# Two-block transformer kernel: GpSimd residual held behind a weight remainder, first loads in two pieces, convolution taps redistributed

## The reference, cut to what matters

```python
# layer 0: RWKV-7 time mix, layer 1: causal attention with rotary embedding ("MoBA")
x = layer_norm(ALPHA * x + mixer(x), ln_mix_g, ln_mix_b)
x = layer_norm(ALPHA * x + (silu(x @ w_gate) * (x @ w_up)) @ w_down, ln_ffn_g, ln_ffn_b)
# time mix, its head: six mixes of x with its predecessor
xx = time_shift(x) - x
xr, xw, xk, xv, xa, xg = [x + xx * mu[n] for n in range(6)]
# second block
n = rmsnorm(h);  c_a, c_g, q, k, v, qi, ki, wi, gc, ga = split(n @ w_in)
u = conv31(c_a * sigmoid(c_g))                # 31 taps per channel, causal, depthwise
score = sum_h wi_h * relu(qi_h . ki)          # 8 index heads
keep  = top 64 keys of each query by score    # mask for the attention over q, k, v
h = h + (sig(gc) * conv_out(u) + sig(ga) * attn_out(attention)) @ w_mix
```

## Time and profile before

| | us |
|---|---|
| median of 3 runs | 1421.13 (1420.81 to 1423.71) |
| profiled execution: its own time | 1424.44 |
| profiled execution: span of its instructions | 1422.2 |
| PE busy in the span | 1337.4 |
| DVE busy | 886.6 |
| ACT busy | 604.2 |
| POOL busy | 66.3 |

### The profile page before, as it was taken

The page is one execution under the profiler, slowest core; times in us unless marked ns, Lnnn a source line. Parts: engine busy times, 40 slices in busy tenths (PEclk is TensorE's granted clock), DMA queues, the critical chain, the costliest instruction groups (busy, mean ns, idle before and its releaser), DMA issues.

```text
span 1422.2 us, 20846 instructions
## 1 busy us (share of the span) xinstructions
PE 1337.4 (94%) x8852; PEld 1192.5 (84%) x8852; DVE 886.6 (62%) x1353; ACT 604.2 (42%) x866; POOL 66.3 (5%) x44
## 2 busy tenths in 40 slices
PE   7999999999999999998999998999988987799998
PEld 3687889879999977767999998989887976699997
DVE  5267776585444475556554447989988655555555
ACT  1432233454344444445433445434345535544443
POOL 0021000030000031002000001000000000000000
PEclk9999999999999999999999999989999999899999
DMA  9333000248555554221755655544533452265650
GB/s 291 128 108 134 14 1 1 102 136 266 180 195 188 178 167 159 97 81 60 264 181 179 189 193 163 151 149 148 160 126 105 143 182 85 86 203 190 200 166 30
DMA packets 154525, 205.59 MB, mean 145 GB/s; under 512 B 7456, under 2 KB 128416, under 8 KB 154304
## 3 DMA queue, kind: packets, MB, share of 16 engines
q1 hardware_dynamic: 154432, 204.25, 44.0%
HBM read 203.19 MB, written 1.05 MB: 144 GB/s over the span
## 4 chain that ended last, share of the span: by engine, by line
PE 72%; DVE 21%; ACT 4%; issue 1%; DMA 0%; DVEq 0%; SPq 0%; ACTq 0%
PE PS L496 18%; PE PS L497 17%; PE PS L498 17%; DVE PH L2332 6%; DVE WW L1790 5%; PE PS L821 4%; PE PS L716 2%; DVE AL L1829 2%; PE PS L858 1%; PE PS L660 1%; ACT WW L1271 1%; PE PS L877 1%; PE PS L884 1%; DVE PA L2036 1%; PE PS L680 1%
## 5 line engine op out<-in xcount | busy, mean ns | idle before, releaser
L1790 DVE TENSOR_TENSOR WW<-RG,WW 128x2048 fp32r<-128x2048 f32 x164 | 374.3, 2289 | 208.6 <-ACT WW L1271 208.4
L496 PE MATMUL PS<-AH,WW 128*128 128x256 f32 x1664 | 479.8, 288 | 14.4 <-DVE AL L1829 9.6
L497 PE MATMUL PS<-AL,WW 128*128 128x256 f32 x1664 | 475.1, 286 | 0.0
L498 PE MATMUL PS<-AH,WW 128*128 128x256 f32 x1664 | 474.7, 285 | 0.0
L1271 ACT ACTIVATE WW<-RG 128x2048 fp32r<-128x2048 f32 x164 | 311.4, 1906 | 92.3 <-PE PS L498 89.7
L496 PEld LDWEIGHTS PS<-AH,WW 128*128 128x128 f32 x1664 | 323.5, 194 | 20.9 <-issue 12.8
L497 PEld LDWEIGHTS PS<-AL,WW 128*128 128x128 f32 x1664 | 323.8, 195 | 1.7 <-issue 0.2
L498 PEld LDWEIGHTS PS<-AH,WW 128*128 128x128 f32 x1664 | 323.6, 194 | 0.0
L496 PE MATMUL PS<-WW,HH 128*128 128x512 f32 x304 | 118.8, 391 | 0.1
L497 PE MATMUL PS<-WW,HH 128*128 128x512 f32 x304 | 118.7, 390 | 0.0
L498 PE MATMUL PS<-WW,HL 128*128 128x512 f32 x304 | 118.3, 389 | 0.0
(11 more groups left out here) (308 smaller groups left out, 1587.3 us busy)
## 6 DMA issues: line engine op xcount, KB each, us to landing
RG<-in_ffn_w_in SPq DMA_DIRECT2D x44, 1024.0 KB, 5.1
RG<-in_w_ff SPq DMA_DIRECT2D x32, 1024.0 KB, 5.3
RG<-in_w_in SPq DMA_DIRECT2D x30, 1024.0 KB, 5.2
RG<-in_ffn_w_down SPq DMA_DIRECT2D x22, 1024.0 KB, 5.0
RG<-in_w_rkv SPq DMA_DIRECT2D x12, 1024.0 KB, 5.0
RG<-in_moba_w_qkv SPq DMA_DIRECT2D x12, 1024.0 KB, 5.3
RG<-in_w_o SPq DMA_DIRECT2D x4, 1024.0 KB, 7.8
RG<-in_wx_kv SPq DMA_DIRECT2D x4, 1024.0 KB, 5.1
```

The source lines that it names most:

```text
L496: e.matmul(o, lh, rh, start=start, stop=False)
L497: e.matmul(o, lh, rl, start=False, stop=False)
L498: return e.matmul(o, ll, rh, start=False, stop=stop)
L1790: v.tensor_tensor(WL[lo_n % NW], ring(SPLIT[lo_n]), WH[lo_n % NW].bitcast(F32), ALU.subtract).then_inc(s_lo, 1)
```

## The change

Four edits, in all five programs where they matter:

1. The first loads: `VB` is loaded in two parts (its first 64 columns, which the mixes and two biases need, then the rest behind `lora`), and `XT` in two halves of four channel tiles, each with a semaphore of its own. DVE starts on the first half.
2. `h_out(q)` waits on POOL for the remainder of the second weight piece of the product that follows: `f0u0`, `mv1s`, `f1u0`.
3. The gains `ln0` and `ln2` move in the ring from in front of `f0g0` (`f1g0`) to behind `f0u0` (`f1u0`), and `ln1` from behind `mkB` to behind `mv1s`. The `ahead` calls that named them name `mkA`, `mkB`, `mvA`.
4. Taps: no portion after `kiwi`; `picks` of 18, 14 and then 11 in place of ten times 10; in the gate steps 7 taps in the first six and 12 in the last two.

```diff
 def ffn_names(f, n, units):
         if j < n:
             out += [f'f{f}{u}{j}' for u in units]
+            if j == 0 and f < 2:
+                out.append(f'ln{2 * f}')
...
-RING = (EARLY + ['wo0', 'wo1', 'wo2', 'wo3', 'mkA', 'ln0'] + ffn_names(0, 11, 'gu') + ['mkB', 'ln1']
-        + ['mv0s', 'mv1s', 'mq0', ...
-           'mo0', 'mo1', 'mo2', 'mo3', 'mvA', 'ln2'] + ffn_names(1, 11, 'gu') + ['mvB', 'ln3']
+RING = (EARLY + ['wo0', 'wo1', 'wo2', 'wo3', 'mkA'] + ffn_names(0, 11, 'gu') + ['mkB']
+        + ['mv0s', 'mv1s', 'ln1', 'mq0', ...
+           'mo0', 'mo1', 'mo2', 'mo3', 'mvA'] + ffn_names(1, 11, 'gu') + ['mvB', 'ln3']
 sync_program (the loads of ln0, ln1, ln2 move with the ring):
-            d.dma_start(VB[:, :], a['vec']).then_inc(s_vec, 16)
-            d.dma_start(XT, a['xT'].rearrange("(k p) t -> p k t", p=128)).then_inc(s_x, 16)
+            d.dma_start(VB[:, 0:64], a['vec'][:, 0:64]).then_inc(s_vec0, 16)
+            for h in range(2):
+                d.dma_start(XT[:, 4 * h:4 * h + 4, :], a['xT'][512 * h:512 * h + 512, :]...).then_inc((s_x, s_x1)[h], 16)
             piece('lora', ...)
+            d.dma_start(VB[:, 64:len(VECS) * 8], a['vec'][:, 64:len(VECS) * 8]).then_inc(s_vec, 16)
 scalar_program (likewise ln1 -> mkB, ln2 -> mvA), vector_program:
-            ahead('ln0', 1)
+            ahead('mkA', 1)
 vector_program:
-            v.wait_ge(s_vec, 16)
+            v.wait_ge(s_vec0, 16)
             v.tensor_scalar(HV[:, 0:16], VB[:, HVI:HVI + 16], 0.5, None, ALU.mult)
-            v.tensor_scalar(HV[:, 16:32], VB[:, HVG:HVG + 16], 0.5, None, ALU.mult)
             v.wait_ge(s_x, 16)
-            own_dve(v.tensor_scalar(XX[:, :, 0:1], XT[:, :, 0:1], -1.0, None, ALU.mult))
+            own_dve(v.tensor_scalar(XX[:, 0:4, 0:1], XT[:, 0:4, 0:1], -1.0, None, ALU.mult))
             for k in range(0, 8, 2):
+                if k == 4:
+                    v.wait_ge(s_x1, 16)
+                    own_dve(v.tensor_scalar(XX[:, 4:8, 0:1], XT[:, 4:8, 0:1], -1.0, None, ALU.mult))
                 mix(0, 1, (k, k + 1))
                 mix(1, 4, (k, k + 1))
+            v.wait_ge(s_vec, 16)
+            v.tensor_scalar(HV[:, 16:32], VB[:, HVG:HVG + 16], 0.5, None, ALU.mult)
...
             for name in ('qi0', 'qi1', 'kiwi'):
                 ahead(name)
-                taps(10)
+                if name != 'kiwi':
+                    taps(10)
...
             for name in [q0..q3, kk0..kk3, va0, va1]:
                 ahead(name)
-                picks(10)
+                picks(18 if name == 'q0' else 14 if name == 'q1' else 11)
...
             for n in range(8):
                 ahead(f'gc{n}' if n < 4 else f'ga{n - 4}', 1 if n == 7 else 2)
                 attention(A2, 2 + n)
-                taps(10)
+                taps(7 if n < 6 else 12)
 gpsimd_program:
             def h_out(q):
                 gains = ring(f'ln{q}')
+                g.wait_ge(s_lo, W[('f0u0', 'mv1s', 'f1u0')[q]] + 1)
                 g.wait_ge(*landed(f'ln{q}'))
```

More of the change, by code:

```diff
@@ L109, in ffn_names @@
     return out
-RING = (EARLY + ['wo0', 'wo1', 'wo2', 'wo3', 'mkA', 'ln0'] + ffn_names(0, 11, 'gu') + ['mkB', 'ln1']
-        + ['mv0s', 'mv1s', 'mq0', 'mk0s', 'mq1', 'mk1s', 'mq2', 'mk2s', 'mv2s', 'mv3s', 'mq3', 'mk3s',
-           'mo0', 'mo1', 'mo2', 'mo3', 'mvA', 'ln2'] + ffn_names(1, 11, 'gu') + ['mvB', 'ln3']
+RING = (EARLY + ['wo0', 'wo1', 'wo2', 'wo3', 'mkA'] + ffn_names(0, 11, 'gu') + ['mkB']
+        + ['mv0s', 'mv1s', 'ln1', 'mq0', 'mk0s', 'mq1', 'mk1s', 'mq2', 'mk2s', 'mv2s', 'mv3s', 'mq3', 'mk3s',
+           'mo0', 'mo1', 'mo2', 'mo3', 'mvA'] + ffn_names(1, 11, 'gu') + ['mvB', 'ln3']
         + [f'c{u}{j}' for j in range(4) for u in 'ag'] + ['qi0', 'qi1', 'kiwi']
@@ L175, in build @@
         s_vo, s_ao, s_go = sem("dve_own"), sem("act_own"), sem("pool_own")
+        s_vec0, s_x1 = sem("mu_in"), sem("xT1_in")
         s_vec, s_x, s_mem, s_cst, s_p2, s_xres, s_out = (
@@ L401, in ffn @@
                             piece(f'f{f}{un}{j}', wcols(w_in, u * 256 * n + 256 * j, 256))
+                        if j == 0 and f < 2:
+                            gains(f'ln{2 * f}', a['lnmg'][f:f + 1, :], a['lnmb'][f:f + 1, :])
                     if j >= 1:
                         piece(f'f{f}d{j - 1}', wcols(w_down, 0, 1024, 2 * (j - 1), 2))
-            d.dma_start(VB[:, :], a['vec']).then_inc(s_vec, 16)
-            d.dma_start(XT, a['xT'].rearrange("(k p) t -> p k t", p=128)).then_inc(s_x, 16)
+            d.dma_start(VB[:, 0:64], a['vec'][:, 0:64]).then_inc(s_vec0, 16)
+            for h in range(2):
+                d.dma_start(XT[:, 4 * h:4 * h + 4, :], a['xT'][512 * h:512 * h + 512, :].rearrange("(k p) t -> p k t", p=128)).then_inc((s_x, s_x1)[h], 16)
             piece('lora', (lambda r: v3(r[:, 0:512], 64), a['w1'].rearrange("(k p) n -> p k n", p=128)),
                   (lambda r: v3(r[:, 512:1024], 64), a['a1'].rearrange("(k p) n -> p k n", p=128)))
+            d.dma_start(VB[:, 64:len(VECS) * 8], a['vec'][:, 64:len(VECS) * 8]).then_inc(s_vec, 16)
             piece('g1', (lambda r: v3(r[:, 0:1280], 160), a['g1'].rearrange("(k p) n -> p k n", p=128)))
@@ L434, in sync_program @@
             piece('mkA', wcols(a['wx_kv'], 0, 256))
-            gains('ln0', a['lnmg'][0:1, :], a['lnmb'][0:1, :])
             ffn(0, 11, 'gu', a['ffn_w_in'][0], a['ffn_w_down'][0])
             piece('mkB', wcols(a['wx_kv'], 256, 256))
-            gains('ln1', a['lnfg'][0:1, :], a['lnfb'][0:1, :])
             M = a['moba_w_qkv']
@@ L442, in sync_program @@
             piece('mv1s', wcols(M, 2048, 512, 4, 4))
+            gains('ln1', a['lnfg'][0:1, :], a['lnfb'][0:1, :])
             for j in range(4):
@@ L451, in sync_program @@
             piece('mvA', wcols(a['wx_kv'], 512, 256))
-            gains('ln2', a['lnmg'][1:2, :], a['lnmb'][1:2, :])
             ffn(1, 11, 'gu', a['ffn_w_in'][1], a['ffn_w_down'][1])
@@ L1593, in scalar_program @@
             ffn(0, True)
-            ahead('ln1', 1)
+            ahead('mkB', 1)
             layer_norm(1)
@@ L1636, in scalar_program @@
             ahead('mo2')
-            ahead('ln2', 1)
+            ahead('mvA', 1)
             layer_norm(2)
@@ L1894, in ln_token @@
                 ln_scale(q, 0)
-                ahead(f'ln{q}', 1)
+                ahead(('mkA', 'mkB', 'mvA')[q], 1)
                 piece_done(first)
```

## The result

| | us |
|---|---|
| kernel before, median of 15 runs | 1421.14 (1416.59 to 1427.80) |
| kernel after, median of 15 runs | 1414.47 (1413.53 to 1421.54) |
| ratio after to before | 0.9959, interval 0.9944 to 0.9974 |
| predicted | 1413.9, range 1408 to 1419 |
| profiled execution of after: own time, span | 1413.63, 1411.8 |

The changed kernel is 6.7 us, 0.41%, faster; the interval leaves no change out. Where those 10.4 come from is read first from single rows at which both kernels do the same thing. Each line of this table gives such a place, when each kernel reaches it, how far after is ahead by then, and how much of that was won or lost since the line above.

What follows compares the result with a forecast made beforehand. The prediction took the kernel as a weight stream through PE with holes (PE 72% of the chain, DVE 21%). Its terms, -1.8 - 5.0 - 3.0 + 2 x 1.3 = -7.2, gave 1413.9 us from a median of 1421.1, range 1408 to 1419.

Steps and rivals of the forecast that it cites:

- First loads: At the start, half of x lands at 4.7 instead of 6.74, so PE's product ends earlier: -1.8 us.
- Norms 0 and 2: Behind these norms, 3.2 gained, then given back by a 2.8 stop before f0u1 and half clock: +1.3 us each.
- Norm 1: PE starts mv1s at 517.6 instead of 520.86 and keeps full clock: -5.0 us.
- The turns: Behind norms 0 and 2, DVE remainders and POOL's four 2.24 us instructions alternate, so f0u1 is ready only at 333.0.
- Rival A: Behind norms 0 and 2 DVE passes POOL: -2.5 per norm, 1406.3 us; chance 0.17 with the halfway case.
- the halfway case: Behind norms 0 and 2 only the clock doesn't fall: 1410.7 us; shares the 0.17 chance of Rival A.
- Taps: Scores 2.5 earlier, DVE 2.8 late at the attention, five gate steps 1.15 shorter each (5.75): -3.0 us in sum.
- rival B: Gate steps stay at 8.7, held by ACT's chain and PE, and the 2.8 lateness remains: 1419.7 us; chance 0.13.
- PE's 7.57: In the gate steps, PE's own step, 8.72 - 1.15 = 7.57, sets the pace once DVE's falls to 7.53.
- Rival C: At the start, the first half of x doesn't land early, the halves sharing DMA engines: +1.8, 1415.7 us; chance 0.08.
- Rival D: In pieces kk1 to vb1, PE's 0.8 waits halve its clock; with 22 us of it, 1424.9 us; chance 0.05.
- faster by more: Whole kernel faster by more than 0.2% (2.8 us): the likeliest case, Rival A, Rival C and half of rival B; chance 0.87.

Runs made afterwards that it cites:

- e1: Kernel before with only the first loads in parts (VB in two parts, XT in two halves); 1420.56 us, ratio 0.9991.
- e2: Kernel before with only POOL's wait for the second remainder and the gains moved in the ring; 1419.74 us, ratio 0.9981.
- e4: Changed kernel with a look ahead of 3 places instead of 2 behind f0u0 and f1u0, on ACT and DVE; 1407.86 us, ratio 0.9897.
- e5: Kernel before with only the gains moved in the ring, without POOL's new wait; 1421.75 us, ratio 0.9994.
- e3: Kernel before with only the taps redistributed; 1420.20 us, ratio 0.9989.
- e7: e4 with three taps back behind kiwi and six instead of seven in the first six gate steps; 1406.66 us, ratio 0.9893.
- e8: Changed kernel with POOL's four residual instructions of 1024 columns cut into eight of 512; 1415.29 us, ratio 0.9951.
- e6: Kernel before with only POOL's wait for the second remainder, the gains left where they were; 1433.47 us, ratio 1.0083.

## Why the prediction was right, and where its steps were off

- **First loads**, -1.8 predicted, -1.3 in both traces (17.93 to 16.61, and 16.53 in e1). The half was there at 5.36 and not at 4.7: the interpolation between 2.8 and 5.5 was 0.7 too hopeful. What it did bring, 1.38, DVE's row of mixes passed on to PE nearly whole.
- **Norms 0 and 2**, +1.3 each; +1.14 and +1.15 measured. The mechanism and its terms were right: stop 2.8 predicted and 2.61 found, clock 1.6 predicted and 1.7 found where it fell (not in every run: e2 once without). e4 shows that this was the short look ahead together with POOL, e5 that the look ahead alone does nothing. (The terms as written, 333.0 against 333.4 and 1.6 of clock, give +1.2 and not +1.3.)
- **Norm 1**, -5.0; -4.8 measured, stop 3.44 to 0.37, with the clock kept. The 0.64 that after lost between norms 1 and 2 had no term in the sum; 0.47 of it stands at the stretch of 644 and the rest stays open.
- **The turns.** HL was put down as waiting for POOL, and did (2.40 for 0.69). Rival A, DVE passing POOL, is out; so is the halfway case. Issue order doesn't speak for rival A either: in the earlier trace rows POOL's instruction of 316.35 stood waiting before DVE could issue its own at 316.9.
- **Taps**, -3.0; -3.65 in the profile, -1.5 with an interval from -3.4 to +0.1 in the times of e3. The step fell to 7.53 as forecast, so rival B is out. DVE took 70.3 from the first remainder behind the scores (944.06) to the last one ahead of the attention (1014.39), which is what the sum of remainders, picks and taps had given. It came there 2.3 late, set against before, and not 2.8, because the scores ended 3.1 earlier and not 2.5; the prediction had named 3.5 for the case that the half clock of the scores goes, and it went. That PE's 7.57 takes over was wrong: subtracting a wait of 1.15 from 8.72 does not give PE's own step, as e7's 7.14 shows. Here nothing hung on it, since DVE's step lay at 7.53 anyway.
- **What e3's times lack.** Behind the attention all ten kernels have the same code. From the product there to the end the five profiles with the new taps (after, e3, e4, e7, e8) need 325.4 to 327.7, on average 326.9, and the five with the old ones (before, e1, e2, e5, e6) 323.9 to 326.8, on average 324.9. The stretch near 1095 is there in four of the first five and in two of the others. So the taps may give back some 2 us of their 3.7 through PE's clock, which would fit the 1.5 of e3; with one profile of each kernel this is not shown, and the profile of after, the one of its five without that stretch, hides it.
- **Rival C** came half true (the first half at 5.36). **Rival D** is out: from 970 to 1004 PE waits 0.34 to 0.92 at each piece, and its granted clock shows no stretch of 0.50 between 945 and 1015. The one at 1020 to 1024 lies in the attention's first steps, 8.72 apart as before (1019.15 and 1027.87), where DVE sets the pace.

That the sum came within 0.6 of the measured time is in part luck. The loads gave 0.5 less than forecast, 0.6 went between norms 1 and 2, the taps gave 0.65 more in the profile and perhaps 1.5 less in the times, and the interval of the measured gain, 3.7 to 8.0, is much wider than 0.6. What the traces do show is the mechanism of each term. The chances, too, add up only roughly: faster by more comes to 0.885 by its parts and not to 0.87.

What the prediction did not have is that single profiles differ by clock stretches, 3.5 us between these two, half as much as the change. It took savings from the span and subtracted them from the median, which kept that out of the sum.

## What to carry to other kernels

When an engine's side work is moved behind a product, follow the buffer slot it holds: the wait alone cost 0.8% through the loads queued behind that slot. When a piece of a look ahead list is moved, count again how far the list reaches at each call: one place cost 8.6 us here, more than the change gained, and one argument gave it back. The length of a step less the engine's wait in it (7.57 here) is only an upper bound on what that engine needs: the step went down to 7.14. And two single profiles are not to be subtracted before their granted clocks are laid side by side, best with a third kernel that has the same code at that place.

## What the runs showed of the hardware

- DVE and POOL, both with two operands in SBUF, take turns of whole instructions, at each length seen here: DVE's 0.69 became 2.40, POOL's 2.4 became 4.48 with a remainder of 2.29 ahead of it, and POOL's 1.29 became 3.2 to 3.3. The Trainium skill (SBUF — State Buffer, Who interferes with whom) says that issue order, and not the kind of operation, decides who blocks; the trace agrees with the blocking for a whole instruction, and shows besides that one who has waited goes before the next of the other, so that two engines with work queued take turns.
- The same instructions met stretches at 0.50 granted clock in one run and none in another (146, 156, 873 and 1095 in before). Behind the stop of 3.44 at norm 1 the clock fell in all four profiles that have it (before, e1, e3, e5), behind those of 2.6 in three of four (after, e2), behind those of 0.4 at norm 1 in none of six. In the scores it fell in all five profiles with PE's stop of 2.26 and in none of the four without the ten taps. A stretch cost 1.7 behind `f0u1`, 1.4 at 1095 (31.7 and 33.1 over the same instructions), some 1.5 at 156 (248.4 and 249.9), 0.4 at 873 and nothing to be seen near 145.
